# First block's attention with stationary values, two heads on the halves of the array's columns, and weights divided before they are turned

## The reference, cut to what matters

```python
s_loc = jnp.einsum('bqkgd,bskd->bkgqs', qb, kb) * scale
s_loc = jnp.where(ok, s_loc, NEG)
s_ctx = jnp.einsum('bqkgd,bckd->bkgqc', qb, k_ctx) * scale
p = jax.nn.softmax(jnp.concatenate([s_loc, s_ctx, s_sink], -1), -1)
return (jnp.einsum('bkgqs,bskd->bqkgd', p_loc, vb)
        + jnp.einsum('bkgqc,bckd->bqkgd', p_ctx, v_ctx))
```

## Time and profile before

| | us |
|---|---|
| median of three executions (2286.06 to 2287.71) | 2286.29 |
| span of the profiled execution, which is its own time | 2288.9 |
| TensorE busy | 2188.9 (96%) |
| VectorE busy | 1238.6 (54%) |
| ScalarE busy | 847.1 (37%) |
| GpSimd busy | 358.4 (16%) |

### The profile page before, as it was taken

One profiled execution on the slowest core, in us unless ns is written; L12 is line 12 of the kernel. 1 busy time (PEld: TensorE's weight loads), 2 busy tenths in 40 slices (PEclk: granted clock), 3 DMA queues, 4 the chain that ended last, 5 costly groups with the idle time before them and its releaser, 6 DMA issues.

```text
span 2288.9 us, 28099 instructions
## 1 busy us (share of the span) xinstructions
PE 2188.9 (96%) x10757; PEld 1671.8 (73%) x10757; DVE 1238.6 (54%) x2370; ACT 847.1 (37%) x1493; POOL 358.4 (16%) x276
## 2 busy tenths in 40 slices
PE   7999998799998999999999999999999999999999
PEld 4786776543436767778788888877677787888887
DVE  4744557621326876675544334469667755453442
ACT  4444544311105455443432222344654433231231
POOL 0111124010002544320000000045433200000000
PEclk9999999889999999999999999999999999999999
DMA  8217301699992222212233232232222122323222
GB/s 303 66 47 230 129 29 48 251 385 409 409 407 87 74 74 56 82 57 65 84 110 101 94 99 92 81 91 83 66 64 82 51 81 92 102 92 101 92 86 80
DMA packets 175580, 288.01 MB, mean 126 GB/s; under 512 B 13486, under 2 KB 125656, under 8 KB 175448
## 3 DMA queue, kind: packets, MB, share of 16 engines
q1 hardware_dynamic: 173152, 278.73, 36.2%
q0 software_dynamic: 1152, 4.19, 0.5%
q10 hardware_dynamic: 1144, 3.29, 0.4%
HBM read 281.98 MB, written 4.19 MB: 125 GB/s over the span
## 4 chain that ended last, share of the span: by engine, by line
PE 80%; DVE 10%; DMA 3%; ACT 3%; issue 2%; SPq 1%; POOL 0%; DVEq 0%; ACTq 0%
PE PS L686 21%; PE PS L688 20%; PE PS L687 20%; PE PS L2496 4%; PE PS L1487 3%; PE PS L2537 2%; PE PS L1469 2%; PE PS L2557 1%; PE PS L1479 1%; SPq L3701 1%; DMA AR<-in_w_mod_dram 1%; DVE AL L868 1%; PE PS L1121 1%; PE PS L1667 1%; DVE CO L865 1%
## 5 line engine op out<-in xcount | busy, mean ns | idle before, releaser
L686 PE MATMUL PS<-OPH,WHI 128*128 128x512 f32 x1192 | 482.0, 404 | 5.5 <-DVE AR L1318 2.8
L688 PE MATMUL PS<-OPH,WLO 128*128 128x512 f32 x1192 | 467.7, 392 | 0.0
L687 PE MATMUL PS<-OPL,WHI 128*128 128x512 f32 x1192 | 466.5, 391 | 0.0
L637 ACT ACTIVATE WHI<-RAW 128x1024 fp32r<-128x1024 f32 (+2 forms) x282 | 292.9, 1041 | 457.4 <-PE PS L688 449.5
L658 DVE TENSOR_TENSOR WLO<-RAW,WHI 128x1024 fp32r<-128x1024 f32 (+1 forms) x187 | 224.3, 1202 | 368.7 <-ACT WHI L637 368.3
L674 POOL TENSOR_TENSOR WLO<-RAW,WHI 128x1024 fp32r<-128x1024 f32 (+1 forms) x95 | 229.8, 2422 | 928.9 <-ACT WHI L637 922.8
L686 PEld LDWEIGHTS PS<-OPH,WHI 128*128 128x128 f32 x1192 | 225.2, 189 | 61.0 <-issue 10.1
L688 PEld LDWEIGHTS PS<-OPH,WLO 128*128 128x128 f32 x1192 | 224.8, 189 | 48.5
L687 PEld LDWEIGHTS PS<-OPL,WHI 128*128 128x128 f32 x1192 | 225.5, 189 | 42.2 <-issue 1.0
L686 PE MATMUL PS<-WHI,OPH 128*128 128x512 f32 (+2 forms) x568 | 226.6, 399 | 9.0 <-DVE OPL L2196 2.5
L688 PE MATMUL PS<-WHI,OPL 128*128 128x512 f32 (+2 forms) x568 | 216.0, 380 | 0.0
(11 more groups left out here) (469 smaller groups left out, 3314.6 us busy)
## 6 DMA issues: line engine op xcount, KB each, us to landing
RAW<-in_w_in_dram SPq DMA_DIRECT2D x102, 512.0 KB, 3.7
RAW<-in_w_ffn_in_dram SPq DMA_DIRECT2D x88, 512.0 KB, 3.5
RAW<-in_w_ffn_out_dram SPq DMA_DIRECT2D x40, 512.0 KB, 3.4
RAW<-in_w_mod_dram SPq DMA_DIRECT2D x36, 512.0 KB, 4.7
ONCE<-in_w_down_dram SPq DMA_DIRECT2D x35, 512.0 KB, 15.8
RX<-in_w_gate_dram SPq DMA_DIRECT2D x29, 512.0 KB, 15.4
RAW<-in_w_out_dram SPq DMA_DIRECT2D x24, 512.0 KB, 3.4
RAW<-in_w_up_dram SPq DMA_DIRECT2D x20, 512.0 KB, 15.7
```

Of the source, the lines that this page charges most:

```text
L637: hi.up(A.e.activation(q.fhi, q.flat, ACT.Copy), ("w", q.i))
L686: T.e.matmul(o, a[0], b[0], start=first, stop=False)
L687: T.e.matmul(o, a[0], b[1], start=False, stop=False)
L688: return T.e.matmul(o, a[1], b[0], start=False, stop=last)
```

## The change

Three things. (1) The values are the stationary operand now, 64 columns of them, and 128 columns of turned weights move; the output comes out turned, 64 rows by 128 tokens. The even head of a pair goes to the left half of the array's columns, the odd one to the right half, and their matmuls alternate (`pe_pair_values`). Pairs are done in odd steps from 5 on. (2) The weights are divided by their sum while they are still in rows, on ScalarE (`evened`), before they are turned; VectorE makes the two divisors of a pair in even steps (`dve_over1`). The turns move one step back, to unit s-3. Weights and turned weights share one buffer, six deep. (3) The outputs need no turns any more: VectorE copies a block's output, and high and low part are made from that copy (`value_split1`).

```diff
+                u.p = u.pt = PB1[:, u.no % 6, 0:u.n]
+                hp = 64 * (h % 2)
+                u.o = PS[hp:hp + 64, 512 * OUT + 128 * (h // 2):512 * OUT + 128 * (h // 2) + 128]
...
+        def pe_pair_values(pair_):
+
+            for u in pair_:
+                T.wait_ge(*copied["pt", u.full])
+            n = len(pair_[0].vs)
+            for j in range(n):
+                for u in pair_:
+                    mm = T.e.matmul(u.o, u.vs[j], u.pt[:, 128 * j:128 * j + 128], start=(j == 0), stop=(j == n - 1))
+            weighed.up(mm, *[u.full for u in pair_])
...
+        def value_split1(who, blk):
+
+            c = slice(128 * blk, 128 * blk + 128)
+            held = YR1[blk].rearrange("p (g n) -> p g n", g=4)
+            if who == "a":
+                A.wait_ge(*tidy["a1", blk])
+                A.wait_ge(*prod["mo", 3])
+                split_a.up(A.e.activation(OPH[:, 0:4, c], held, ACT.Copy), ("a1", blk))
+            else:
+                V.wait_ge(*split_a["a1", blk])
+                split_v.up(V.e.tensor_tensor(OPL[:, 0:4, c], held, OPH[:, 0:4, c].bitcast(F32), ALU.subtract), ("a1", blk))
...
(pe_att1)
-                    if s >= 3:
-                        T.wait_ge(*copied["pt", att1[s - 3].name])
+                    if s >= 4:
+                        T.wait_ge(*copied["pt", att1[s - 4].name])
...
-                if 2 <= s < 34:
-                    u = att1[s - 2]
-                    T.wait_ge(*expd[u.name])
+                if 3 <= s < 35:
+                    u = att1[s - 3]
+                    T.wait_ge(*evened[u.name])
...
-                if s >= 3:
-                    u = att1[s - 3]
-                    if u.h == 0 and u.blk:
+                if s >= 5 and s % 2:
+                    u = att1[s - 4]
+                    if u.h == 1 and u.blk:
                         T.wait_ge(*tidy["a1", u.blk - 1])
-                    pe_values(u, u.name)
-                for blk in TURNS1.get(s, ()):
-                    pe_block_turned(("a1", blk), YR1[blk], tidy["a1", blk], D)
+                    pe_pair_values(att1[s - 5:s - 3])
...
(dve_att1)
+                if 2 <= s < 34 and s % 2 == 0:
+                    dve_over1(att1[s - 1])
...
+                if 3 <= s < 35:
+                    u = att1[s - 3]
+                    if u.no % 2:
+                        copy_pt(u, u.name)
+                if 4 <= s < 36:
+                    u = att1[s - 4]
                     if u.h == 7:
-                        dve_tidy1(u.blk)
+                        V.wait_ge(*weighed[u.name])
+                        tidy.up(V.e.tensor_copy(YR1[u.blk], ps(OUT)), ("a1", u.blk))
...
(act_att1)
                 if 2 <= s < 34:
                     u = att1[s - 2]
+                    A.wait_ge(*tidy["over", u.no])
+                    evened.up(A.e.activation(u.p, u.p, ACT.Copy, scale=u.over), u.name)
+                if 3 <= s < 35:
+                    u = att1[s - 3]
                     if u.no % 2 == 0:
-                        if u.no >= 2:
-                            A.wait_ge(*weighed[att1[u.no - 2].name])
                         copy_pt(u, u.name)
...
(pe_cells)
-            pe_block_turned(("a1", 3), YR1[3], tidy["a1", 3])
```

More of the change, by code:

```diff
@@ L417, in body @@
     least, expd, sank, tidy = signal("least"), signal("expd"), signal("sank"), signal("tidy")
+    evened = signal("evened")
     gate_v, gate_a = signal("gate_v"), signal("gate_a")
@@ L1429, in programs @@
             off = 0
[L1431 to L1432 removed]
+        PB1 = in_(AR1, 14712, 3840).rearrange("p (i n) -> p i n", i=6)
         YR1 = [in_(AR1, 18552 + 512 * i, 512) if i < 2 else in_(AR2, 2048 + 512 * i, 512) for i in range(4)]
@@ L1457, in programs @@
                 u.name = ("a1", u.no)
-                u.p, u.pt = PB1[:, u.no % 4, 0:u.n], PTB1[:, u.no % 2, 0:u.n]
-                u.o = ps(OUT)[:, 64 * h:64 * h + 64]
+                u.p = u.pt = PB1[:, u.no % 6, 0:u.n]
+                hp = 64 * (h % 2)
+                u.o = PS[hp:hp + 64, 512 * OUT + 128 * (h // 2):512 * OUT + 128 * (h // 2) + 128]
+                u.over, u.full = a8[:, 32 + h:33 + h], u.name
                 u.at = 1024 if u.n == 512 else 896
@@ L1645, in pe_att1 @@
             dense = pe_between1()
-            for s in range(35):
+            for s in range(36):
                 if s < 32:
@@ L1685, in dve_att1 @@
             V.wait_ge(*set_v["sink"])
-            for s in range(36):
+            for s in range(37):
+                if 2 <= s < 34 and s % 2 == 0:
+                    dve_over1(att1[s - 1])
                 if s < 32:
@@ L1690, in dve_att1 @@
                         V.wait_ge(*tidy["a1", u.blk - 2])
-                    if u.no >= 4:
-                        V.wait_ge(*turned["pt", att1[u.no - 4].name])
+                    if u.no >= 6:
+                        V.wait_ge(*weighed[att1[u.no - 6].name])
                     dve_least(u, u.name, u.p)
@@ L1715, in dve_att1, with dve_over1 @@
                 pass
[L1717 to L1720, removed]
+        def dve_over1(u):
+            a8, h = AC8[:, u.blk % 2, :], u.h - 1
+            V.wait_ge(*sank["a1", u.blk, u.h])
+            t = tidy.up(V.e.tensor_tensor(a8[:, 24 + h:26 + h], a8[:, 8 + h:10 + h], a8[:, 16 + h:18 + h], ALU.add))
             V.wait_ge(*t)
[L1722 to L1727, removed]
+            tidy.up(V.e.reciprocal(a8[:, 32 + h:34 + h], a8[:, 24 + h:26 + h]), ("over", u.no - 1), ("over", u.no))
         def act_att1():
@@ L1749, in act_att1 @@
                 for blk in TURNS1.get(s, ()):
-                    act_block_split(("a1", blk), OPH[:, 0:4, 128 * blk:128 * blk + 128])
+                    value_split1("a", blk)
                 next(gates, None)
@@ L1987, in act_cells @@
                               turned[name, c])
-            act_block_split(("a1", 3), OPH[:, 0:4, 384:512])
+            value_split1("a", 3)
             cb = PB["col"]
@@ L2042, in pool_cells @@
             pool_lo(J["out"][0][2] + 1)
-            G.wait_ge(*turned["blk", ("a1", 3)])
+            G.wait_ge(*weighed["a1", 31])
             for k in KEYS:
@@ L2069, in dve_cells @@
                               turned[name, c])
-            dve_block_split(("a1", 3), OPL[:, 0:4, 384:512], OPH[:, 0:4, 384:512])
+            value_split1("v", 3)
             V.wait_ge(*copy_a["mo", 3])
```

13 lines of the change are left out of this document (3 added, 10 removed).

## The result

| | before | after |
|---|---|---|
| median of the runs, us | 2287.0 (4 runs) | 2319.68 (2317.31 to 2321.46) |
| ratio to before | | 1.0133 (1.0119 to 1.0147) |
| span of the profiled execution | 2288.9 | 2318.2 |

The change is slower, as forecast, but by 33 us (2319.7 against 2287.0) and not by 20; 2307 was forecast and the range ended at 2314. The measured time lies beyond it.

The account below looks back on a forecast made before the run. TensorE paces the attention steps, but VectorE's copy of turned weights already sets the next step's start. 3.5 + 12.9 + 0 + 4 = 20.4 us on 2288.9 gives 2309.3, as median 2306.7, said 2307; range 2295 to 2314.

Parts of the forecast that it names:

- Even steps gain nothing: Even attention steps: scores again 1.15 us behind the turns' end, nothing gained; 0.6 us lost over steps 20 to 30.
- ScalarE's queue in odd steps: Odd steps: exp, sink's exp, division, copy precede the scores; 3.8 us against 3.1, 2.6 lost over steps 21 to 29.
- The pair's 1.3 us: Values of two heads on TensorE: 1.27 us a pair, against 2.12 for two heads before; bounds 1.07 and 2.34.
- the overlap of the halves: Values on TensorE: two column halves run two abreast, 0.107 us for 128 columns, as in the experts' products.
- the third rival: Values: halves don't overlap with 128 columns, a pair takes 2.34 us instead of 1.27; +9, 2315 us; chance 0.07.
- The five late places: Delays from queues in steps 2, 6, 10, 16, 18: +4.0, +0.9, +3.6, +2.5, +1.9 us, together 12.9.
- The first rival: Attention waits are one unlucky lining-up; only 3.5 us steady and 4.0 at the start are paid; 2294 us; chance 0.08.
- Clock: TensorE's clock falls behind new waits before scores 4, 12, 17: 1.3 us each, +4 (0 to 8).
- the shift passes through: Behind the attention stage: experts' weights are requested only as it frees their places, so its delay carries on; no extra time.
- The end of the stage: Last copy behind VectorE's two splits, last values 3.4 us later; until 328.62 net -0.2, taken as 0, bounds -2 and +3.
- the steady part: Attention steps' regular loss from even steps, odd steps and changing array parts: 3.5 us, bounds 1 and 5.
- The second rival: Turned weights arrive before TensorE asks, copy ending within 0.6 us of the turns; TensorE's 12 us won; 2276; chance 0.09.

Follow-up runs that it names:

- serial: Changed kernel with the two heads of a pair one after the other in their column halves, not alternating; ratio 1.0134, median 2321.0 us.
- copyfirst: Changed kernel with ScalarE's copy of turned weights at the head of its step, ahead of exp, sink's exp and division; ratio 1.0100, median 2310.1 us.
- shift: Changed kernel with ScalarE's other work (high parts, silus, logarithm) one step later; ratio 1.0079, median 2307.7 us.
- dvefirst: Changed kernel with VectorE's copy of turned weights ahead of its convolution steps (7, 9, 15, 16); ratio 1.0114, median 2314.9 us.
- poolwait: Changed kernel with GpSimd's two additions waiting until VectorE's low part of block 2 is done; ratio 1.0121, median 2316.4 us.
- tail: Changed kernel with VectorE's low parts of blocks 0 to 2 made in the next stage; ratio 1.0114, median 2312.7 us.
- banks: Changed kernel where scores skip the wait for the last copy of turned weights if both units have 512 keys; ratio 1.0103, median 2312.9 us.
- combo2: Changed kernel with five reordering edits together, plus ScalarE's convolutions heading their steps and sigmoids behind the last division; ratio 1.0046, median 2300.2 us.

## Why the forecast was too small

**Even steps gain nothing: right.** Scores wait 0.87 to 0.92 for VectorE's copy, where the values lay.

**ScalarE's queue in odd steps: right in kind and size.** 3.71 for 3.8. The division starts its successor after 0.72 (0.74 estimated). The pair's 1.3 us (group length; 1.27 forecast) and the overlap of the halves were right too, so the third rival falls. Its price of +9 was too high: `serial`, where it is made true, lengthens the odd steps by 4.4.

**The five late places: right.** 13.0 for 12.9, though the sum is closer than its terms: the third is 0.6 over its forecast and the fourth 0.6 under. `copyfirst`, `shift` and `dvefirst` take them away by the edits that the theory names. The first rival falls. (By its own rows the third of the five is 3.7, not 3.6.)

**Clock: the mechanism right, the size too small.** 4 was put at 1.3 each for three places. It was four places, 7.7 together, since step 17 ran wholly at the lower level (3.1). How much of it falls due is partly luck: `poolwait`, the same program up to there, ran step 12 in 4.8 instead of 6.3.

**Clock behind the stage: no term in the sum.** The sum has "the shift passes through" there, and nothing was added. It measured -2.3 + 3.6. The 3.6 is three stretches at the lower level where the kernel before ran the same instructions at 1.00: at 378 (1.6 us), at 784 (1.6) and at 1572 (1.5, of which a later wait takes up 1.0). The last two are missing in `tail` and `copyfirst`, which lose 0.3 and 0.8 behind the second broadcasts. No experiment was made for them; they are read from the traces alone, and why the clock fell there and not elsewhere stays open.

**The end of the stage: wrong.** "Until 328.62 I get -0.2; I take 0, bounds -2 and +3." It measured +6.4. The step that failed is "VectorE's two splits ahead of its last copy": the order was right, but the sum gave the splits nothing beyond their own work. The last values were to come 3.4 us later behind scores 31 than before; they came 8.4 later (17.1 against 8.7). The change has this subtraction read two operands in SBUF, beside GpSimd's tensor_tensors, and GpSimd held it. With GpSimd's additions moved (`poolwait`) the last values come 4.2 earlier and +6.4 becomes +2.6; with the low parts moved (`tail`) it becomes -0.8.

So of the 12 us missing, 6.4 arose at the end of the stage (GpSimd's hold is 3.8 of them by `poolwait`), 3.7 are the clock inside the stage, 1.3 the clock behind it, and 0.6 the steady part and the late places.

The trace of before had the sign. Beside GpSimd's products, an addition of 128x8 elements took 0.94 (0.16 in its three other places), and it ended with them (315.03 + 4.98 = 320.01, 319.08 + 0.94 = 320.02). The low parts, which then read PSUM and SBUF, took 0.69 and 0.68 beside the same products, as if alone:

```profile
315.03 4.98 POOL L1420 TENSOR_TENSOR AR<-AR,RB 128x512 f32<-128x512 f32 x4 [7.70 <-ACT AR L1619]
...
317.88 1.29 DVE L1526 TENSOR_TENSOR OPL<-PS,OPH 128x512 fp32r<-128x512 f32 x2 [3.27 <-ACT OPH L1519]
...
319.08 0.94 DVE L1720 TENSOR_TENSOR AC<-AC 128x8 f32<-128x8 f32 x1
```

The Trainium skill has the rule: SBUF — State Buffer, section "SBUF: two separate sides", says that VectorE and GpSimd share a pair of ports, taken as an exclusive lock for a whole instruction, and that a VectorE operation with two SBUF inputs is subject to it when GpSimd's operation reads SBUF. By that rule the second low part waits until GpSimd lets go, and the traces agree (4.8 us for 0.68 of work, 2.08 for 0.16, 0.68 again once GpSimd's additions are moved, and no hold on the low parts that read PSUM).

**The second rival** (TensorE's 12 us won) named its condition: a copy that ends within 0.6 of the turns. `banks` comes at such a gain by another way, as the scores no longer wait for the copy: steps 28 and 29 take 5.8 us against 7.2 after the change and 6.9 before it. In the blocks of 640 keys, where turned weights and the next scores share a bank, this can't be done.

## What to carry to other kernels

Before pricing an operation that moves from PSUM to SBUF operands, look at which engine works beside it: VectorE with two SBUF inputs beside GpSimd took seven times its own duration (4.8 us for 0.68), and a 128x2 addition thirteen times (2.08 for 0.16). Work taken off the busiest engine is worth only what the next event in line allows: here each step ended with a copy that TensorE's values had been hiding. When a copy moves one step back in an in-order queue, list everything that now stands ahead of it in every step, and count each long wait twice: once as the wait and once as slow clock behind it.

## What was not expected of the hardware

A VectorE operation held by GpSimd gets in between some of GpSimd's instructions and not between others. The first low part ended 0.5 behind the products, and GpSimd's first addition then took 1.49 us instead of 1.05, so GpSimd was held in its turn. The second, issued at 341.5 during that addition, let the second addition and the low part of a weight piece go ahead and ran only when the chain of three ended at 345.8. Other traces show the same pair of lengths (1.5 and 4.8 in `copyfirst`, `banks`, `shift` and `dvefirst`, 1.7 and 4.8 in `combo2`).

The clock fell behind the waits of 2.3 to 7.2 us in steps 4, 12, 17 and 20, and stayed at 1.00 where TensorE waited 0.9 in every second step (steps 21 to 30). How much it costs behind one and the same wait is not fixed (0.66 and 0.91 above), and it fell 400 and 1200 us behind the stage at places where it had not fallen before; that noise is as large as several terms of the sum.
